# Six stages of a float32 transformer kernel take their first two output pairs by halves of the inputs

## The chip, the cores and the metric

One core of one Trainium2 chip runs the whole program in one launch. The metric is the device time of one execution in microseconds, as the median of several; lower is better.

## The reference

Batch 1, 256 tokens, width 2048, all in float32. A first block of two layers, then a second block of one layer. Cut to the matrix products, which are most of the work (`rms` is a root-mean-square norm):

```python
for l in range(2):                                   # first block
    proj = rms(x) @ w_in[l]                          # 56 tiles of 128 columns
    mixed = [short_gated_conv(...), diff_attention(...), memory_attention(mem @ w_mem_kv[l])]
    x = x + concat(mixed) @ w_out[l]
# second block
h = rms(x) * (1 + sc1) + sh1                         # modulation: silu(c) @ w_mod + b_mod
proj = h @ w_in_2
o_a = sliding_window_attention(...); o_b = gated_linear_attention(...)
merged = sigmoid(g_a) * (o_a @ w_branch_attn) + sigmoid(g_b) * (o_b @ w_branch_gla)
x = x + g1 * rms(merged @ w_out_2)
h = rms(x) * (1 + sc2) + sh2
x = x + g2 * rms((silu(gate) * val) @ w_down)        # gate, val = conv(h @ w_up)
```

## The kernel before, in words

**Stages, pairs, units.** Every matrix product is a stage. They run one after another: mem0, mem1, qkv0, heads0a to c, out0, qkv1, heads1a to c, out1, q_a, and so on to g_b, branch_a, branch_b, mix_out, up0, down0, up1, down1. A stage makes its output in pairs of tiles. A pair needs all 16 tiles of the input, and takes them in `per_pair` steps. One step is a unit: 512 KB of weights (`UK` = 4 input tiles by 256 output columns; in a token stage `WK` = 2 input tiles by 512 columns) and the matmuls on them. mem1, out0, qkv1 and branch_b have 4 units to a pair; out1 and mix_out are token stages, in which the input is the stationary operand, with 8. A turn is `body` = 2 pairs (in token stages the loop goes over pairs directly).

**Float32 from halves.** Each float32 value is split into a rounded high part and the rest. The weights of a unit land in `RAW`; ScalarE writes the high part `WH` (`act_split`, L540), VectorE the rest `WL` (`dve_split`, L549), and TensorE multiplies (L468 and L473; in token stages L415 to L417). ScalarE and VectorE split four units ahead: at unit w of a stage, `split_ahead` splits unit w+4, into one of `RING` = 4 slots, once unit w is done. The count of splits goes by the unit's place in the stage.

**Input chunks.** The input `XH` of a stage is prepared in four chunks of four tiles (`act_input_chunk`, L1121 and L1127; `dve_input_chunk`, L1138 and L1146). `xh_ready` counts them, and TensorE waits for chunk q in the first pair only, at unit q (at units 2q and 2q+1 in a token stage). The first chunks are prepared beside the last units of the stage before (`inside`), the others behind its last evacuation.

**Banks and evacuation.** Pairs alternate between two halves of the accumulator `ACC` in PSUM: an even pair uses banks 0 and 1, an odd one banks 2 and 3. At the end of a pair ScalarE copies one part to `HIGH` (L804), and VectorE adds (L938 and L940; L950, L953, L956, L961 in the stages with a sum), which raises `evacuated`. A pair may start when the pair two before it is evacuated:

```python
wait_from_zero(pe, k.evacuated, i * stage.body + (stage.pair0 + b - 1))   # first unit of pair b
```

**Order.** Each engine has its program written out in order; all run the same loop over pairs and units, and each does for unit w its split ahead, its side work for that place (sums, memory keys at L1473, attention of another stage, a modulation step L1932 on VectorE), and at a pair's end the evacuation. SP issues the loads of weights (`RAW`) and of modulation (`RAWMOD`) in one fixed sequence, five buffers deep: a load waits until the one five before it is used. In mem1 the column sums of four chunks (L1084) stand behind unit 1, in qkv1 those of the last chunk (L1061) behind unit 3.

Of the kernel before, what the change touches and what calls it, by code (L numbers as in the profile page):

```python
# [11 lines left out]
P = 128  # L12
# [20 lines left out]
NORMED = ("out1", "mix_out", "down1")  # L33
WARM = 32
# [63 lines left out]
class Stage:  # L98


    def __init__(self, name, source, per_pair, pairs, body, inputs, kind, dst, tiles=2,
# [12 lines left out]
        assert pairs % body == 0 and self.units % RING == 0  # L114

# [172 lines left out]

def end_unit(stage):

    return stage.unit0 + stage.pairs * stage.per_pair
# [15 lines left out]
def wait_from_zero(engine, sem, value):  # L307

    if value > 0:
        engine.wait_ge(sem, value)  # L310

# [8 lines left out]
def program_sync(sp, k):  # L320
# [73 lines left out]
def pe_token_stage(pe, k, stage):  # L394

    operand = k.AH if stage.inputs is None else k.XH
    for j in range(stage.pairs):
        bank0 = 2 * ((stage.pair0 + j) % 2)
        pe.wait_ge(k.evacuated, stage.pair0 + j - 1)
        if stage.name == "mix_out" and j > 1:  # L400
            pe.wait_ge(k.tok_squared, 8 + 2 * (j - 1))
        for q in range(stage.per_pair):
            w = j * stage.per_pair + q
            if stage.inputs is not None and j == 0:
                pe.wait_ge(k.xh_ready, stage.inputs + q * WK // UK + 1)
            if stage.inputs is None and j == 0:
                pe.wait_ge(k.evacuated, stage.pair0 - WK * (stage.per_pair - q - 1))
            pe.wait_ge(k.split_ready, stage.unit0 + w + 1)
            high, low = wide(k.WH[:, w % RING]), wide(k.WL[:, w % RING])
            for b in range(2):  # L410
                bank = k.ACC[:, bank0 + b]
                for kc in range(WK):
                    tile = WK * q + kc
                    x = operand[:, tile, b * P:b * P + P]
                    pe.matmul(bank, x, high[:, kc], start=tile == 0, stop=False)  # L415
                    pe.matmul(bank, x, low[:, kc], start=False, stop=False)  # L416
                    mm = pe.matmul(bank, operand[:, tile, T + b * P:T + b * P + P], high[:, kc],  # L417
                                   start=False, stop=tile == WK * stage.per_pair - 1)
                if b == 0 and q == stage.per_pair - 1:
                    mm.then_inc(k.half_done, 1)  # L420
            mm.then_inc(k.unit_done, 1)
            pe_beside(pe, k, stage, j, q)
            if stage.name == "out1" and (j, q) == (1, 7):
                pe_rotary(pe, k)
            if stage.name == "down1" and j == 0 and q in (1, 3, 5, 7):
                pe_gain_rows(pe, k, 1, q // 2)
# [21 lines left out]
def pe_stage(pe, k, stage):  # L448
# [27 lines left out]
    def turn(i, last):  # L476
        for b in range(stage.body):
            bank0 = 2 * ((stage.pair0 + b) % 2)

            wait_from_zero(pe, k.evacuated, i * stage.body + (stage.pair0 + b - 1))  # L480
            if stage.name == "up0" and (i, b) == (0, 0):
                pe_first_tiles(pe, k, stage)
                continue
            for q in range(stage.per_pair):
                w = b * stage.per_pair + q
                by_tile = stage.inputs in (k.plan.h2, k.plan.f_in)
                if stage.inputs is not None and b == 0 and not by_tile:
                    pe.wait_ge(k.xh_ready, stage.inputs + q + 1)
                if stage.inputs is None and b == 0:
                    pe.wait_ge(k.evacuated, stage.pair0 - UK * (stage.per_pair - q - 1))  # L490
                pe.wait_ge(k.split_ready, i * stage.units + (stage.unit0 + w + 1))
                for n in range(0, UK * stage.tiles, 2):
                    both = [operands(bank0, q, n + a) for a in range(2)]
                    if stage.name == "q_a" and (i, b) == (0, 0):
                        if both[0][3] + 4 < KT:
                            pe_turn_normed(pe, k, 0, both[0][3] + 4)
                        pe.wait_ge(k.xh_ready, stage.inputs + both[1][3] + 1)
                    high(both[0], w)
                    high(both[1], w)
                    low(both[0], w)  # L500
                    mm = low(both[1], w)
                mm.then_inc(k.unit_done, 1)
                pe_beside(pe, k, stage, i, w)
                if stage.name == "mem0" and (i, w) == (0, 5):
                    pe.wait_ge(k.consts_ready, 1)
                    for c in range(4):
                        presummed_sums(pe, k, 0, c)
                if stage.name == "mem1" and (i, w) == (0, 1):
                    pe.wait_ge(k.rstd_ready, 1)
                    for c in range(4):  # L510
                        presummed_sums(pe, k, 1, c)
                if stage.name == "mem1" and (i, w) == (0, 3):
                    pe_memory_keys(pe, k, 0)
                if stage.name == "qkv0" and (i, w) == (0, 5):
                    pe_memory_keys(pe, k, 1)
                if stage.name == "qkv0" and (i, w) == (1, 1):
                    pe.wait_ge(k.mk_ready, 2)
                if stage.name == "qkv1" and i > 0 and w == 1:
                    pe_turn_residual(pe, k, i - 1)
                if stage.name == "kv_a" and w == 1:  # L520
                    pe_decays(pe, k)
                if stage.name == "g_b" and w == 5:
                    pe_gain_rows(pe, k, 0, i)
                if stage.norm is not None and b % 2 == 1 and q == 1 and i * stage.body + b > 1:
                    presummed_sums(pe, k, stage.norm, (i * stage.body + b) // 2 - 1)
                if stage.sums_last is not None and w == 3 and i == 0:
                    chunk_sums(pe, k, stage.sums_last, 3)
# [35 lines left out]
def act_token_stage(act, k, stage, chain):  # L563

    for j in range(stage.pairs):
        last_pair = j == stage.pairs - 1
        for q in range(stage.per_pair):
            w = j * stage.per_pair + q
            late = stage.name in ("out1", "mix_out") and last_pair and q == stage.per_pair - 1
            if not late:  # L570
                token_split_ahead(act, k, stage, w, act_split)
            act_beside(act, k, stage, j, q, chain)
            if stage.name == "out1" and (j, q) == (2, 5):
                act_rotary(act, k)
            if stage.name == "down1" and j == 0 and q in (2, 4, 6, 8):
                act_gain_rows(act, k, 1, q // 2 - 1)
        if stage.name == "down0":
            continue
# [1920 lines left out]
```

## Time and profile before

| | us |
|---|---|
| median of 3 runs | 2597.96 |
| lowest and highest | 2597.32, 2598.81 |
| span of the profiled execution, first to last instruction | 2596.0 |
| TensorE busy in it | 2547.3 |
| VectorE busy in it | 1939.5 |
| ScalarE busy in it | 1300.1 |

The profile is of one execution. It gives the span of that execution and no other time for it, so its own time is at least the 2596.0 us of the span; the median of the runs is 1.96 us above that. The granted clock of TensorE, averaged over the span, is 0.995 of full speed. A matmul's end is modelled, and matmuls overlap, so the start times are what to go by.

### The profile page before, as it was taken

Reading aid. Unit: us, or ns where it says so; the run is one execution under the profiler, and the core shown is the slowest. Engines: PE = TensorE matmul, PEld = TensorE weight load, DVE = VectorE, ACT = ScalarE, POOL = GpSimd, SP = SyncE. Lnnn points to the kernel's source line nnn. Section 1 sums busy time; section 2 is a strip of 40 time slices with the busy share of each in tenths; the row PEclk is TensorE's granted clock in tenths of the full one; section 3 lists DMA queues with packets and bytes.
Section 4 is the critical chain, followed back from the end, with each engine's and each line's share of the span. In section 5 each row is a group of like instructions: output and inputs, shape, how many; then the busy total and the mean of one; then the engine's idle time right before and its main releaser. Section 6 shows DMA issues by size and latency. Waiting matters only on the chain.

```text
span 2596.0 us, 35319 instructions
## 1 busy us (share of the span) xinstructions
PE 2547.3 (98%) x13936; PEld 2175.1 (84%) x13936; DVE 1939.5 (75%) x2769; ACT 1300.1 (50%) x1758; POOL 10.8 (0%) x62
## 2 busy tenths in 40 slices
PE   7999999999999999999999999999999999999998
PEld 6888888888888887888788888888888888888886
DVE  6877766887777687676667787887788887788855
ACT  7544555554455555454444554544644443444443
POOL 0000000000000010000000000000000000000000
PEclk9999999999999999999999999999999999999999
DMA  8687554778754466755567788888476668976764
GB/s 271 219 299 244 160 154 143 228 258 286 242 158 152 149 214 218 235 171 154 153 190 222 231 277 277 270 282 272 143 197 189 188 208 307 284 203 196 201 194 140
DMA packets 526519, 556.64 MB, mean 214 GB/s; under 512 B 17409, under 2 KB 453762, under 8 KB 526226
## 3 DMA queue, kind: packets, MB, share of 16 engines
q1 hardware_dynamic: 526354, 554.38, 68.4%
q8 instruction: 110, 1.80, 0.3%
q14 instruction: 55, 0.45, 0.1%
HBM read 552.22 MB, written 2.10 MB: 214 GB/s over the span
## 4 chain that ended last, share of the span: by engine, by line
PE 88%; DVE 7%; ACT 3%; issue 1%; DMA 0%; DVEq 0%; SPq 0%; ACTq 0%
PE ACC L468 43%; PE ACC L473 21%; PE ACC L415 6%; PE ACC L417 6%; PE ACC L416 6%; DVE WL L549 2%; PE OU L1268 1%; ACT WH L540 1%; PE SC L1235 1%; PE SC L1247 1%; ACT PROB L1293 1%; PE SC L1276 1%; DVE XH L1138 0%; DVE XH L1146 0%; DVE PROB L1352 0%
## 5 line engine op out<-in xcount | busy, mean ns | idle before, releaser
L468 PE MATMUL ACC<-XH,WH 128*128 128x512 f32 x5296 | 1692.3, 401 | 21.2 <-DVE XH L1146 15.3
L540 ACT ACTIVATE WH<-RAW 128x1024 fp32r<-128x1024 f32 (+1 forms) x852 | 897.9, 1057 | 1166.5 <-PE ACC L473 836.1
L549 DVE TENSOR_TENSOR WL<-RAW,WH 128x1024 fp32r<-128x1024 f32 (+1 forms) x852 | 1032.6, 1220 | 568.5 <-ACT WH L540 567.0
L473 PEld LDWEIGHTS ACC<-XH,WL 128*128 128x128 f32 x5296 | 998.7, 189 | 236.6
L473 PE MATMUL ACC<-XH,WL 128*128 128x256 f32 x5296 | 1044.2, 279 | 0.0
L468 PEld LDWEIGHTS ACC<-XH,WH 128*128 128x128 f32 x5296 | 814.4, 189 | 41.2 <-issue 18.5
L1932 DVE SCALAR_TENSOR_TENSOR RAWMOD<-RAWMOD,CSILU 128x1024 f32<-128x1024 f32 x192 | 233.8, 1218 | 1.0 <-DMA RAWMOD<-in_w_mod_t 0.7
L415 PE MATMUL ACC<-WH,XH 128*128 128x512 f32 x384 | 151.9, 396 | 3.6 <-DVE WL L549 3.6
L416 PE MATMUL ACC<-WL,XH 128*128 128x512 f32 x384 | 149.6, 390 | 0.0
L417 PE MATMUL ACC<-WH,XH 128*128 128x512 f32 x384 | 149.5, 389 | 0.0
L415 PE MATMUL ACC<-WH,AH 128*128 128x512 f32 x352 | 137.3, 390 | 0.0
L417 PE MATMUL ACC<-WH,AH 128*128 128x512 f32 x352 | 137.0, 389 | 0.0
L416 PE MATMUL ACC<-WL,AH 128*128 128x512 f32 x352 | 137.0, 389 | 0.0
L415 PEld LDWEIGHTS ACC<-WH,XH 128*128 128x128 f32 x384 | 72.1, 188 | 22.1 <-issue 7.5
L804 ACT ACTIVATE HIGH<-ACC 128x512 f32<-128x512 f32 (+1 forms) x171 | 89.9, 526 | 0.0
L417 PEld LDWEIGHTS ACC<-WH,XH 128*128 128x128 f32 x384 | 72.1, 188 | 15.3
L416 PEld LDWEIGHTS ACC<-WL,XH 128*128 128x128 f32 x384 | 72.1, 188 | 14.4
L417 PEld LDWEIGHTS ACC<-WH,AH 128*128 128x128 f32 x352 | 66.1, 188 | 13.8
L416 PEld LDWEIGHTS ACC<-WL,AH 128*128 128x128 f32 x352 | 66.1, 188 | 13.5
L415 PEld LDWEIGHTS ACC<-WH,AH 128*128 128x128 f32 x352 | 66.1, 188 | 13.5
L938 DVE TENSOR_TENSOR PR<-ACC,HIGH 128x512 f32<-128x512 f32 x64 | 43.7, 682 | 3.6 <-ACT HIGH L804 3.6
L979 DVE SCALAR_TENSOR_TENSOR CV<-U,PARAM,CV 128x256 f32<-128x256 f32 x88 | 42.7, 485 | 3.1
(287 smaller groups left out, 1438.0 us busy)
## 6 DMA issues: line engine op xcount, KB each, us to landing
RAW<-in_w_in SPq DMA_DIRECT2D x408, 512.0 KB, 4.5
RAWMOD<-in_w_mod_t SPq DMA_DIRECT2D x192, 512.0 KB, 4.9
RAW<-in_w_up SPq DMA_DIRECT2D x176, 512.0 KB, 4.7
RAW<-in_w_out SPq DMA_DIRECT2D x96, 512.0 KB, 5.4
RAW<-in_w_down SPq DMA_DIRECT2D x88, 512.0 KB, 5.0
RAW<-in_w_mem_kv SPq DMA_DIRECT2D x32, 512.0 KB, 5.8
RAW<-in_w_branch_gla SPq DMA_DIRECT2D x32, 512.0 KB, 5.1
RAW<-in_w_branch_attn SPq DMA_DIRECT2D x16, 512.0 KB, 5.2
```

The lines of the kernel that those rows point to most:

```text
L415: pe.matmul(bank, x, high[:, kc], start=tile == 0, stop=False)
L416: pe.matmul(bank, x, low[:, kc], start=False, stop=False)
L417: mm = pe.matmul(bank, operand[:, tile, T + b * P:T + b * P + P], high[:, kc], start=False, stop=tile == WK * stage.per_pair - 1)
L468: return pe.matmul(bank, k.WH[:, w % RING, kc, cols], x, start=tile == 0, stop=False)
L473: return pe.matmul(bank[:, 0:T], k.WL[:, w % RING, kc, cols], x[:, 0:T], start=False, stop=tile == tiles - 1)
L540: act.activation(k.WH[:, slot, :, 0:width], k.RAW[:, r % RAWS, :, 0:width], ACT.Copy).then_inc(k.hi_ready, 1)
L549: dve.tensor_tensor(k.WL[:, slot, :, 0:width], k.RAW[:, k.plan.unit_load[unit] % RAWS, :, 0:width], k.WH[:, slot, :, 0:width].bitcast(F32) ...
L804: act.activation(k.HIGH[:, first:stage.tiles], k.ACC[:, bank + first:bank + stage.tiles, T:2 * T], ACT.Copy).then_inc(k.high_ready, 1)
L938: chain.link(dve.tensor_tensor(dst, low, high, ALU.add))
L979: dve.scalar_tensor_tensor(out=cv, in0=u[:, 0:T], scalar=column(taps[0]), in1=cv, op0=ALU.mult, op1=ALU.add).then_inc(done, 1)
L1235: mm = pe.matmul(k.SC[:, c, b * T:b * T + T], q, keys, start=True, stop=True)
L1932: dve.scalar_tensor_tensor(out=raw, in0=raw, scalar=1.0, in1=k.CSILU[:, half * MOD_COLS:(half + 1) * MOD_COLS], op0=ALU.mult, op1=ALU.mult ...
```

## The change

A list names six stages. In each, the first two pairs go by halves of their units: first half of pair 0, first half of pair 1, second half of pair 0, second half of pair 1. Later pairs go as before. All engines and the loads follow the same order. What is done at a place in the stage (the w-th unit: splits, sums, memory keys, modulation) stays at that place; what is done at a pair's end (the copy to `HIGH`, the evacuation) moves with the pair: for the first pair from behind unit 3 to behind unit 5 (token stages: from 7 to 11); the second pair's stays behind unit 7 (15). TensorE's wait for `evacuated` stands at each pair's first unit.

```diff
+HALVED = ("mem1", "out0", "qkv1", "out1", "branch_b", "mix_out")
...
+    def order(self):
+
+        if self.name not in HALVED:
+            return [(b, q) for b in range(self.body) for q in range(self.per_pair)]
+        half = self.per_pair // 2
+        return [(b, part * half + q) for part in range(2) for b in range(2) for q in range(half)]
...
+def stage_order(stage):
+
+    order = stage.order()
+    done = len(order) // stage.per_pair
+    return order + [(j, q) for j in range(done, stage.pairs) for q in range(stage.per_pair)]
+
+
+def pair_end(stage, j):
+
+    return stage.unit0 + stage_order(stage).index((j, stage.per_pair - 1)) + 1
...
+def turn_order(stage, i):
+
+    return stage.order() if i == 0 else [(b, q) for b in range(stage.body)
+                                         for q in range(stage.per_pair)]
...
     for stage in k.stages:
-        for j in range(stage.pairs):
-            for q in range(stage.per_pair):
-                by_unit[stage.unit0 + j * stage.per_pair + q] = (stage, j, q)
+        for w, (j, q) in enumerate(stage_order(stage)):
+            by_unit[stage.unit0 + w] = (stage, j, q)
...
     operand = k.AH if stage.inputs is None else k.XH
-    for j in range(stage.pairs):
+    for w, (j, q) in enumerate(stage_order(stage)):
         bank0 = 2 * ((stage.pair0 + j) % 2)
-        pe.wait_ge(k.evacuated, stage.pair0 + j - 1)
...
+        if q == 0:
+            pe.wait_ge(k.evacuated, stage.pair0 + j - 1)
...
     def turn(i, last):
...
+        for w, (b, q) in enumerate(turn_order(stage, i)):
             bank0 = 2 * ((stage.pair0 + b) % 2)
...
+            if q == 0:
+                wait_from_zero(pe, k.evacuated, i * stage.body + (stage.pair0 + b - 1))
...
+            if stage.inputs is not None and b == 0 and not by_tile:
+                pe.wait_ge(k.xh_ready, stage.inputs + q + 1)
...
+            pe.wait_ge(k.split_ready, i * stage.units + (stage.unit0 + w + 1))
...
+    def copy_high(i, b):
...
+        act.wait_ge(k.unit_done, pair_end(stage, i * stage.body + b))
...
+            if q == stage.per_pair - 1:
+                copy_high(i, b)
...
+            if q == stage.per_pair - 1:
+                evacuate(i, b)
```

TensorE's order at the head of mem1, from the end of unit 1 over the column sums into unit 2. The name in brackets is what a row waits for. Before:

```order
L468 MATMUL ACC<-XH,WH 128x512 x2
L473 MATMUL ACC<-XH,WL 128x256 x2
L1084 MATMUL OU<-PR,ONES 128x256 [waits presummed,rstd_ready]
L1084 MATMUL OU<-PR,ONES 128x256 [waits presummed] x3
L468 MATMUL ACC<-XH,WH 128x512 [waits split_ready,xh_ready]
L468 MATMUL ACC<-XH,WH 128x512
```

And now (the file's lines have moved, L492 is the former L468, L1115 the former L1084):

```order
L492 MATMUL ACC<-XH,WH 128x512 x2
L497 MATMUL ACC<-XH,WL 128x256 x2
L1115 MATMUL OU<-PR,ONES 128x256 [waits presummed,rstd_ready]
L1115 MATMUL OU<-PR,ONES 128x256 [waits presummed] x3
L492 MATMUL ACC<-XH,WH 128x512 [waits split_ready,evacuated]
L492 MATMUL ACC<-XH,WH 128x512
```

Unit 2 belonged to the first pair and waited for an input chunk; it now belongs to the second pair and waits for that pair's bank.

VectorE's order in out0 from the splits of its units 4 and 5 on: WL rows are splits, RAWMOD rows modulation steps, the SUM and X rows a pair's evacuation. Before:

```order
L549 TENSOR_TENSOR WL<-RAW,WH 128x1024 [waits hi_ready] x2
L1932 SCALAR_TENSOR_TENSOR RAWMOD,DERIVED<-RAWMOD,CSILU 128x1024 [waits landed3]
L549 TENSOR_TENSOR WL<-RAW,WH 128x1024 [waits hi_ready] x2
L1932 SCALAR_TENSOR_TENSOR RAWMOD,DERIVED<-RAWMOD,CSILU 128x1024 [waits landed1]
L950 TENSOR_TENSOR SUM<-ACC,HIGH 128x512 [waits high_ready]
L961 TENSOR_TENSOR X<-X,SUM 128x512 [waits dve_step]
L549 TENSOR_TENSOR WL<-RAW,WH 128x1024 [waits hi_ready] x2
L1932 SCALAR_TENSOR_TENSOR RAWMOD,DERIVED<-RAWMOD,CSILU 128x1024 [waits landed4]
L549 TENSOR_TENSOR WL<-RAW,WH 128x1024 [waits hi_ready] x2
```

And now (L573 is the former L549, L1963 the former L1932, L982 and L993 the former L950 and L961):

```order
L573 TENSOR_TENSOR WL<-RAW,WH 128x1024 [waits hi_ready] x2
L1963 SCALAR_TENSOR_TENSOR RAWMOD,DERIVED<-RAWMOD,CSILU 128x1024 [waits landed3]
L573 TENSOR_TENSOR WL<-RAW,WH 128x1024 [waits hi_ready] x2
L1963 SCALAR_TENSOR_TENSOR RAWMOD,DERIVED<-RAWMOD,CSILU 128x1024 [waits landed1]
L573 TENSOR_TENSOR WL<-RAW,WH 128x1024 [waits hi_ready] x2
L1963 SCALAR_TENSOR_TENSOR RAWMOD,DERIVED<-RAWMOD,CSILU 128x1024 [waits landed4]
L982 TENSOR_TENSOR SUM<-ACC,HIGH 128x512 [waits high_ready]
L993 TENSOR_TENSOR X<-X,SUM 128x512 [waits dve_step]
L573 TENSOR_TENSOR WL<-RAW,WH 128x1024 [waits hi_ready] x2
```

The first pair's evacuation has moved behind two more splits (units 8 and 9) and one more modulation step.

## Rows read from the trace of the kernel before

**Rows 1.** The page: span, busy time (share) and instructions; two costliest split groups

```profile
span 2596.0 us, 35319 instructions
...
PE 2547.3 (98%) x13936; PEld 2175.1 (84%) x13936; DVE 1939.5 (75%) x2769; ACT 1300.1 (50%) x1758; POOL 10.8 (0%) x62
...
L540 ACT ACTIVATE WH<-RAW 128x1024 fp32r<-128x1024 f32 (+1 forms) x852 | 897.9, 1057 | 1166.5 <-PE ACC L473 836.1
L549 DVE TENSOR_TENSOR WL<-RAW,WH 128x1024 fp32r<-128x1024 f32 (+1 forms) x852 | 1032.6, 1220 | 568.5 <-ACT WH L540 567.0
```

**Rows 2.** TensorE's waits, whole span: released by, us in total, times, longest

```profile
PE ACC L468 <- DVE XH L1146: 15.3, 3, 11.1
...
PE ACC L415 <- DVE WL L549: 3.6, 2, 2.8
```

**Rows 3.** Timeline of TensorE, head of qkv1: start, us, row, idle before and releaser

```profile
567.00 0.63 PE L468 MATMUL ACC<-XH,WH 128*128 128x512 f32 x2
...
569.78 0.63 PE L468 MATMUL ACC<-XH,WH 128*128 128x512 f32 x2
...
575.14 0.73 PE L468 MATMUL ACC<-XH,WH 128*128 128x512 f32 x2 [2.41 <-DVE XH L1146]
...
579.60 1.89 PE L1061 MATMUL SC<-PR,ONES 128*128 128x256 f32 x8
581.13 0.81 PE L468 MATMUL ACC<-XH,WH 128*128 128x512 f32 x2
```

**Rows 4.** Timeline of TensorE, out0: starts of units 2, 3 and 4

```profile
477.23 0.63 PE L468 MATMUL ACC<-XH,WH 128*128 128x512 f32 x2
...
481.97 0.73 PE L468 MATMUL ACC<-XH,WH 128*128 128x512 f32 x2 [1.80 <-DVE XH L1138]
...
484.87 0.63 PE L468 MATMUL ACC<-XH,WH 128*128 128x512 f32 x2
```

**Rows 5.** Timeline of VectorE, out0

```profile
477.33 0.69 DVE L940 TENSOR_TENSOR PR<-PR,RSTD 128x512 f32<-128x512 f32 x1
...
483.00 2.36 DVE L549 TENSOR_TENSOR WL<-RAW,WH 128x1024 fp32r<-128x1024 f32 x2 [1.08 <-ACT WH L540]
...
491.68 2.60 DVE L549 TENSOR_TENSOR WL<-RAW,WH 128x1024 fp32r<-128x1024 f32 x2
494.19 1.22 DVE L1932 SCALAR_TENSOR_TENSOR RAWMOD<-RAWMOD,CSILU 128x1024 f32<-128x1024 f32 x1
```

**Rows 6.** Timeline of TensorE, mem1: unit 1, the sums, unit 2

```profile
66.40 0.73 PE L468 MATMUL ACC<-XH,WH 128*128 128x512 f32 x2 [1.77 <-DVE XH L1146]
...
70.85 1.89 PE L1084 MATMUL OU<-PR,ONES 128*128 128x256 f32 x8
72.39 0.81 PE L468 MATMUL ACC<-XH,WH 128*128 128x512 f32 x2
```

**Rows 7.** Timeline of VectorE: last evacuations before mem1 and before qkv1

```profile
74.54 0.69 DVE L940 TENSOR_TENSOR PR<-PR,RSTDM 128x512 f32<-128x512 f32 x1
...
570.95 0.69 DVE L961 TENSOR_TENSOR X<-X,SUM 128x512 f32<-128x512 f32 x1
```

**Rows 8.** Timelines of VectorE and TensorE, out1, unit 4 and its split

```profile
941.01 2.36 DVE L549 TENSOR_TENSOR WL<-RAW,WH 128x1024 fp32r<-128x1024 f32 x2 [1.07 <-ACT WH L540]
...
942.38 0.47 PE L415 MATMUL ACC<-WH,XH 128*128 128x512 f32 x1 [2.77 <-DVE WL L549]
```

**Rows 9.** Windows: length, busy (count) of PE, PEld, DVE, ACT, POOL; PEclk, DMA share, GB/s

```profile
67.30:70.70 3.40, 3.40 (x12) 2.81 (x11) 3.33 (x8) 1.56 (x3) 0.00 (x0) 0.50 0.44 154
...
575.90:579.30 3.40, 3.40 (x12) 2.90 (x12) 3.40 (x5) 1.27 (x2) 0.00 (x0) 0.50 0.43 127
```

**Rows 10.** Timelines around branch_b: last evacuation before it, unit 2, a modulation step

```profile
1665.94 0.69 DVE L953 TENSOR_TENSOR PR<-PR,SUM 128x512 f32<-128x512 f32 x1
...
1668.25 0.63 PE L468 MATMUL ACC<-XH,WH 128*128 128x512 f32 x2
...
1681.89 1.22 DVE L1932 SCALAR_TENSOR_TENSOR RAWMOD<-RAWMOD,CSILU 128x1024 f32<-128x1024 f32 x1
```

More of the change, by code:

```diff
@@ L396, in pe_token_stage @@
     operand = k.AH if stage.inputs is None else k.XH
-    for j in range(stage.pairs):
+    for w, (j, q) in enumerate(stage_order(stage)):
         bank0 = 2 * ((stage.pair0 + j) % 2)
-        pe.wait_ge(k.evacuated, stage.pair0 + j - 1)
-        if stage.name == "mix_out" and j > 1:
+        if q == 0:
+            pe.wait_ge(k.evacuated, stage.pair0 + j - 1)
+        if q == 0 and stage.name == "mix_out" and j > 1:
             pe.wait_ge(k.tok_squared, 8 + 2 * (j - 1))
[L402 to L426, printed above, removed]
@@ L429, in pe_first_tiles @@
+        mm.then_inc(k.unit_done, 1)
+        pe_beside(pe, k, stage, j, q)
+        if stage.name == "out1" and (j, q) == (1, 7):
+            pe_rotary(pe, k)
+        if stage.name == "down1" and j == 0 and q in (1, 3, 5, 7):
+            pe_gain_rows(pe, k, 1, q // 2)
 def pe_first_tiles(pe, k, stage):
@@ L476, in turn @@
     def turn(i, last):
-        for b in range(stage.body):
+        if stage.name == "up0" and i == 0:
+            pe.wait_ge(k.evacuated, stage.pair0 - 1)
+            pe_first_tiles(pe, k, stage)
+        for w, (b, q) in enumerate(turn_order(stage, i)):
             bank0 = 2 * ((stage.pair0 + b) % 2)
-            wait_from_zero(pe, k.evacuated, i * stage.body + (stage.pair0 + b - 1))
             if stage.name == "up0" and (i, b) == (0, 0):
-                pe_first_tiles(pe, k, stage)
                 continue
[L484 to L527, printed above, removed]
@@ new lines, in turn @@
+            for n in range(0, UK * stage.tiles, 2):
+                both = [operands(bank0, q, n + a) for a in range(2)]
+                if stage.name == "q_a" and (i, b) == (0, 0):
+                    if both[0][3] + 4 < KT:
+                        pe_turn_normed(pe, k, 0, both[0][3] + 4)
+                    pe.wait_ge(k.xh_ready, stage.inputs + both[1][3] + 1)
+                high(both[0], w)
+                high(both[1], w)
+                low(both[0], w)
+                mm = low(both[1], w)
@@ new lines, in turn @@
+            mm.then_inc(k.unit_done, 1)
+            pe_beside(pe, k, stage, i, w)
+            if stage.name == "mem0" and (i, w) == (0, 5):
+                pe.wait_ge(k.consts_ready, 1)
+                for c in range(4):
+                    presummed_sums(pe, k, 0, c)
+            if stage.name == "mem1" and (i, w) == (0, 1):
+                pe.wait_ge(k.rstd_ready, 1)
+                for c in range(4):
+                    presummed_sums(pe, k, 1, c)
+            if stage.name == "mem1" and (i, w) == (0, 3):
+                pe_memory_keys(pe, k, 0)
@@ L529, in pe_stage @@
+            if stage.sums_last is not None and w == 3 and i == 0:
+                chunk_sums(pe, k, stage.sums_last, 3)
     stage_turns(stage, turn)
@@ new lines, in dve_token_stage @@
+        late = stage.name in ("out1", "mix_out") and last_pair and q >= stage.per_pair - 2
+        if not late:
+            token_split_ahead(dve, k, stage, w, dve_split)
+        unit = stage.unit0 + w
+        if unit in k.plan.mod_adds:
+            dve_modulation_sums(dve, k, k.plan.mod_adds[unit], chain)
+        for n in k.plan.mod_steps.get(unit, ()):
+            dve_modulation(dve, k, n)
+        dve_beside(dve, k, stage, j, q, chain)
+        if stage.name == "out1" and (j, q) == (1, 5):
+            dve_rotary(dve, k)
```

331 lines of the change are left out of this document (173 added, 158 removed).

## The prediction

> **What bounds the kernel now.** I read the page first: TensorE is busy for 98% of the span [rows 1], so only its gaps, its clock and work put on its path can move the time. Then the list of who waited for whom for TensorE: it waited for input chunks (VectorE's XH) and for weight splits (VectorE's WL) [rows 2]; 11.1 us of the first is the start of the program. Then TensorE's timeline at the head of each of the six stages, beside VectorE's. A unit takes 2.79 us: two neighbours start at 567.00 and 569.78 [rows 3]. I number a stage's units from 0. The waits at the heads are:
> - mem1, unit 1: 1.77 us [rows 6].
> - out0, unit 3: 1.80 us [rows 4].
> - qkv1, unit 3: 2.41 us [rows 3].
> - out1, unit 4: 2.77 us [rows 8], and mix_out, unit 4: the rest of the 3.6 us that two waits for WL make, 0.8 us [rows 2].
>
> A gap can cost twice. After the waits of 1.77 and 2.41 us the granted clock was 0.50 (1.2 GHz) for 3.4 us [rows 9]. In qkv1 unit 3 ran from 575.14 to the column sums at 579.60, so 4.46 us where 2.79 are normal: 1.67 us lost [rows 3].
>
> **What the change does to each head.** Unit 0 and 1 stay the first pair's. Units 2 and 3 become the second pair's first half, 4 and 5 the first pair's second half. Two things follow. Input chunks 2 and 3 are wanted two units later, in token stages four. But the second pair's bank is wanted two units earlier, so unit 2 now waits until the last pair of the stage before is evacuated.
>
> *mem1.* Unit 2 started at 72.39, right behind eight sum matmuls from 70.85; it waited for nothing [rows 6]. The wait of unit 1 is for chunk 1, which the new order still wants there. So nothing is removed. What is added: the last pair of mem0 is evacuated by VectorE's L940, which starts at 74.54 and takes 0.69 us, so it ends at 75.23 [rows 7]. Unit 2 starts about 75.25 in place of 72.39, 2.86 us later. Of that some 0.1 us comes back, since unit 2 of before was still slowed at its start. Cost: **+2.75 us**, and nothing behind takes it up: the later heads' chunks and evacuations wait for TensorE's own units, so they move along with it.
>
> *out0.* Unit 2 would start at 477.23 [rows 4]; the bank is free when L940, from 477.33, has ended at 478.02 [rows 5]: 0.8 us of new wait. Units 2 and 3 then end at 478.05 + 2 x 2.79 = 483.63. Unit 4 needs no late chunk, but its weights: VectorE's split starts at 483.00, and of the two in 2.36 us the first ends about 484.2 [rows 5]. Unit 4 so starts at 484.2, not at 484.87 [rows 4]: 0.67 us gained, not 1.80. Then unit 8, the third pair, wants the first pair's bank. That pair now ends with unit 5 and not 3, and VectorE reaches its evacuation behind two splits from 491.68 and the modulation step of 494.19 (1.22 us), so from 495.33; two steps of 0.69 us end at 496.7 [rows 5]. Unit 8 would start at 484.2 + 4 x 2.79 = 495.36, and before it was 484.87 + 11.16 = 496.03. So it starts at 496.7: **+0.7 us** over before. The 0.67 us are given back, and the same again.
>
> *qkv1.* Unit 2 would start at 569.78 [rows 3]; out0's last evacuation, L961 from 570.95, ends at 571.64 [rows 7]. New wait 1.9 us. Unit 3 follows at 574.5, by when chunk 3 is not wanted; the sums come at 577.3 and take 1.53 us (579.60 to 581.13), unit 4 starts at 578.8 in place of 581.13 [rows 3]. **-2.35 us**: 0.7 because a wait of 1.9 stands for one of 2.6 between starts, 1.67 from the clock, if that stays at 2.4 GHz. At unit 8 the first pair's evacuation is in time: behind unit 5 come a ScalarE split of 1.06, a VectorE split of 1.22 [rows 1] and two steps of 0.69, 3.7 us, where two units give 5.58.
>
> *out1.* Unit 4 waits for its split, not for a chunk: VectorE's WL rows start at 941.01, the first ends about 942.2, and TensorE goes on at 942.38 [rows 8]. Weights are split by the unit's place in the stage, whichever pair it serves. The wait stays whole: **0**. *mix_out* is the same with 0.8 us [rows 2]: **0**.
>
> *branch_b.* Its late chunks are 0 and 1, wanted at units 0 and 1 in either order. The bank for unit 2 is free at 1666.63 (L953) [rows 10], and unit 2 started at 1668.25: no wait. At unit 8, due at 1668.25 + 6 x 2.79 = 1685.0, VectorE has the modulation step of 1681.89 (1.22 us) and then three evacuation steps of some 0.7 us: 1685.2 [rows 10]. **+0.25 us**.
>
> No instruction, byte or DMA is added; the loads are the same number in the same places of SP's queue, only with other columns. I cost that at 0; a stall would show as ScalarE's splits waiting for DMA.
>
> Sum at full clock: 2.75 + 0.7 - 2.35 + 0 + 0 + 0.25 = +1.35 us.
>
> **The clock.** The change makes two new waits, about 2.5 us in mem1 and 1.9 us in qkv1. Of the four waits of this size that I listed, those of 1.77 and 2.41 us were followed by half clock, those of 1.80 and 2.77 us were not [rows 3, 4, 6, 8, 9]. So each new one costs 0 or 1.67 us, and I take one of the two: +1.67. Forecast: +3.0 us over the median of 2597.96, so **2601.0 us**. The sum is made against the profiled execution with its span of 2596.0 us [rows 1]; the median of the three runs is 1.96 us above that span, and I carry that over. A measurement here can tell a change of about 0.2%, 5.2 us, from none.
>
> The Trainium skill's page "TensorE: Matmul & The Clock Gate", section "HAM oscillation — how this bites in real kernels", advises to do all K-tiles of one output tile before waiting, so that TensorE stays warm. [...]
>
> **The rivals.**
> - *Both new waits are followed by half clock*: +1.35 + 2 x 1.67 = +4.7, 2602.7 us. For it: 2.5 us is longer than two waits that were followed by it. Against it: 2.77 us in out1 was not. Or *neither is*: 2599.3 us. [...]
> - *The heads' waits simply vanish* (faster). Then 1.80 + 2.41 + 1.67 + 2.77 + 0.8 = 9.45 us go: 2588.5 us. For it: all these waits stand at units that the change moves. Against it: out1's and mix_out's are for splits, and the two evacuations above lie later than the units that now want them. It holds only if both readings are wrong.
> - *The first pair's evacuation is late at unit 8 in more stages* (slower). VectorE works in order, and the evacuation now has two units of room, 5.58 us, where it had four. In mem1 its queue also holds the memory keys and a modulation step there, in branch_b it is late already. One more VectorE step of 1.2 us in front of it in mem1, qkv1 and branch_b makes 3.6 us: +1.35 + 3.6 + 1.67 = 6.6, 2604.6 us. It decides as soon as the queue is behind by more than the 1.8 us that qkv1 has to spare.
> - That the order is not what the diff says: the listings show it is. No chance given.
>
> **How the numbers follow.** One half-clock period more: 0.35; both: 0.20; neither: 0.15; all three lie within 5.2 us of before. Vanishing waits: 0.10. Late evacuations: 0.20. So faster 0.10, same 0.70, slower 0.20. The range leaves out the vanishing waits (0.1) and the worse half of the late evacuations (0.1): it goes up to 2604.6. Down it goes to 2596.0: 2599.3, less 1.67 if mem1's own half-clock period goes too, less the 1.5 us by which the three runs differ.
>
> **What would show it.** In the changed kernel's profile: at mem1's head a TensorE wait of about 2.5 us released by the evacuation (PR, the former L940) behind the sums, and the old 1.8 us before it; in out0 three short waits (0.8 for PR, 0.5 for WL, 1.3 for X before unit 8) in place of one; in qkv1 1.9 us for X before unit 2 and none before unit 5; out1 and mix_out still 2.8 and 0.8 us for WL. The number of half-clock periods decides within 3.3 us. I am wrong if mem1 shows no wait for PR, or if the WL wait of out1 is gone.

## The result, and the profile of the changed kernel

The changed kernel took 2604.46 us (median of 7 runs, 2601.96 to 2606.76), the kernel before beside it 2597.64 us (7 runs, 2597.14 to 2598.81): a ratio of 1.0022, interval 1.0013 to 1.0031. That is 6.8 us more, where 3.0 were forecast: the sign was right, the size was not. The profiled execution took 2604.52 us, with a span of 2602.8 us against 2596.0 [rows 1].

The page of the changed kernel, its first lines:

```profile
span 2602.8 us, 35319 instructions
...
PE 2551.4 (98%) x13936; PEld 2177.3 (84%) x13936; DVE 1940.0 (75%) x2769; ACT 1300.1 (50%) x1758; POOL 10.8 (0%) x62
```

The number of instructions is that of before, and VectorE's and ScalarE's busy times are within 0.5 us of it. TensorE alone is busy 4.1 us longer with the same matmuls, and the other 2.7 us are gaps. TensorE's waits of the changed kernel over the whole span (released by, us in total, times, longest), those of its unit streams:

```profile
PE ACC L492 <- DVE XH L1177: 12.7, 2, 11.0
...
PE ACC L439 <- DVE WL L573: 3.6, 2, 2.8
...
PE ACC L492 <- DVE PR L972: 3.2, 2, 2.5
PE ACC L492 <- DVE X L993: 3.1, 2, 1.8
```

Beside [rows 2]: the chunk waits (XH) have lost qkv1's 2.4 us and out0's 1.8 us, and what is left is the program's start and mem1's 1.7. The split waits (WL) of out1 and mix_out are whole, 3.6 us. New are waits for evacuated banks: 3.2 us for PR, 3.1 us for X. TensorE's timeline at the heads (start, us, row, idle before and releaser):

```profile
70.70 1.89 PE L1115 MATMUL OU<-PR,ONES 128*128 128x256 f32 x8
75.12 0.73 PE L492 MATMUL ACC<-XH,WH 128*128 128x512 f32 x2 [2.53 <-DVE PR L972]
...
480.71 0.73 PE L492 MATMUL ACC<-XH,WH 128*128 128x512 f32 x2 [0.69 <-DVE PR L972]
...
487.02 0.70 PE L492 MATMUL ACC<-XH,WH 128*128 128x512 f32 x2 [0.46 <-DVE WL L573]
...
499.74 0.73 PE L492 MATMUL ACC<-XH,WH 128*128 128x512 f32 x2 [1.34 <-DVE X L993]
...
575.53 1.07 PE L492 MATMUL ACC<-XH,WH 128*128 128x512 f32 x2 [1.75 <-DVE X L993]
...
582.77 1.89 PE L1092 MATMUL SC<-PR,ONES 128*128 128x256 f32 x8
584.31 0.81 PE L492 MATMUL ACC<-XH,WH 128*128 128x512 f32 x2
...
945.53 0.47 PE L439 MATMUL ACC<-WH,XH 128*128 128x512 f32 x1 [2.78 <-DVE WL L573]
```

These waits stand at the units where the prediction had put them: mem1 unit 2, out0 units 2, 4 and 8, qkv1 unit 2, out1 unit 4. In branch_b no wait is listed; unit 8 starts at 1691.65 us, right behind the third evacuation step of 1690.90 (0.69 us). To read what each head costs I took the time from the start of one unit to the next in both traces and summed the differences of a head:

| head | forecast | changed less before |
|---|---|---|
| mem1 | +2.75 | +2.7 |
| out0 | +0.7 | +1.1 |
| qkv1 | -2.35 | -0.7 |
| out1, mix_out | 0 | 0.0 |
| branch_b | +0.25 | +0.3 |
| kv_a | not listed | +3.2 |

They sum to 6.6 of the 6.8 us. Two lines are off by more than half a microsecond, and they are both the clock. In qkv1 the new wait was followed by half clock as the old one was. And kv_a, a stage that the change does not touch, took 3.2 us more in its units 1 and 2. There TensorE does sixteen 16-row matmuls for the decays, in the changed kernel:

```profile
1088.85 1.99 PE L1715 MATMUL SC<-GKL,WUP 16*128 16x256 f32 x8
1090.68 3.16 PE L1715 MATMUL OU<-GKL,WUP 16*128 16x256 f32 x8
1093.77 1.22 PE L492 MATMUL ACC<-XH,WH 128*128 128x512 f32 x2
```

and in the kernel before:

```profile
1085.64 1.99 PE L1684 MATMUL SC<-GKL,WUP 16*128 16x256 f32 x8
1087.48 1.89 PE L1684 MATMUL OU<-GKL,WUP 16*128 16x256 f32 x8
1089.29 0.72 PE L468 MATMUL ACC<-XH,WH 128*128 128x512 f32 x2
```

The first eight are alike, the second eight take 1.81 us before and 3.09 after, from their start to that of the next row. The same window in both (length, busy (count) of PE, PEld, DVE, ACT, POOL; PEclk, DMA share, GB/s), of the changed kernel:

```profile
1091.20:1097.90 6.70, 6.70 (x20) 5.07 (x19) 0.13 (x1) 0.00 (x0) 0.00 (x0) 0.50 0.52 167
```

and of the kernel before:

```profile
1091.20:1097.90 6.70, 6.70 (x40) 5.85 (x40) 4.36 (x9) 1.06 (x1) 0.00 (x0) 1.00 0.31 88
```

At a clock of 0.50, against 1.00 (1.2 GHz against 2.4), TensorE does 20 matmul records in 6.7 us and not 40. Nothing had it waiting ahead of that: it was at work all through, on matmuls with 16 rows. So the question for the runs was whether the change brings this about, or chance does.

### The profile page after: what moved, and what is told of

It is laid out like the page before. It is cut to its first block, busy times and chain, and to the rows that moved or that the text cites. A ratio compares the mean times of both kernels' runs of the same rounds, so it can differ in the third digit from the quotient of the medians.

```text
span 2602.8 us, 35319 instructions
## 1 busy us (share of the span) xinstructions
PE 2551.4 (98%) x13936; PEld 2177.3 (84%) x13936; DVE 1940.0 (75%) x2769; ACT 1300.1 (50%) x1758; POOL 10.8 (0%) x62
## 4 chain that ended last, share of the span: by engine, by line
PE 87%; DVE 8%; ACT 3%; issue 1%; DMA 0%; DVEq 0%; SPq 0%; ACTq 0%
PE ACC L492 43%; PE ACC L497 21%; PE ACC L439 6%; PE ACC L441 6%; PE ACC L440 6%; DVE WL L573 2%; ACT WH L564 1%; PE OU L1299 1%; PE SC L1266 1%; PE SC L1278 1%; ACT PROB L1324 1%; PE SC L1307 1%; DVE XH L1177 0%; DVE RAWMOD L1963 0%; DVE PROB L1383 0%
## 5 line engine op out<-in xcount | busy, mean ns | idle before, releaser
L492 PE MATMUL ACC<-XH,WH 128*128 128x512 f32 x5296 | 1694.3, 401 | 23.8 <-DVE XH L1177 12.7
L573 DVE TENSOR_TENSOR WL<-RAW,WH 128x1024 fp32r<-128x1024 f32 (+1 forms) x852 | 1032.9, 1220 | 575.9 <-ACT WH L564 574.3
L492 PEld LDWEIGHTS ACC<-XH,WH 128*128 128x128 f32 x5296 | 815.4, 190 | 45.0 <-issue 19.5
L1963 DVE SCALAR_TENSOR_TENSOR RAWMOD<-RAWMOD,CSILU 128x1024 f32<-128x1024 f32 x192 | 233.9, 1218 | 2.8 <-DMA RAWMOD<-in_w_mod_t 2.7
L1009 DVE SCALAR_TENSOR_TENSOR CV<-U,PARAM,CV 128x256 f32<-128x256 f32 x88 | 42.7, 485 | 3.1
L1011 DVE SCALAR_TENSOR_TENSOR CV<-U,PARAM,CV 128x256 f32<-128x256 f32 x88 | 42.7, 485 | 3.1
```

The lines of the kernel that those rows point to most:

```text
L492: return pe.matmul(bank, k.WH[:, w % RING, kc, cols], x, start=tile == 0, stop=False)
L573: dve.tensor_tensor(k.WL[:, slot, :, 0:width], k.RAW[:, k.plan.unit_load[unit] % RAWS, :, 0:width], k.WH[:, slot, :, 0:width].bitcast(F32) ...
L1009: chain.link(dve.scalar_tensor_tensor(out=cv, in0=u[:, 1:1 + T], scalar=column(taps[1]), in1=cv, op0=ALU.mult, op1=ALU.add))
L1011: dve.scalar_tensor_tensor(out=cv, in0=u[:, 0:T], scalar=column(taps[0]), in1=cv, op0=ALU.mult, op1=ALU.add).then_inc(done, 1)
L1963: dve.scalar_tensor_tensor(out=raw, in0=raw, scalar=1.0, in1=k.CSILU[:, half * MOD_COLS:(half + 1) * MOD_COLS], op0=ALU.mult, op1=ALU.mult ...
```

## The experiments

**A count of half-clock periods.** A trace records the granted clock. In all of them it falls to 0.50 for 3.4 us at a time (or 6.8, two such periods in a row, as in kv_a above), and a period costs about 1.7 us of TensorE's work. I counted them in each trace, leaving out the one at the program's end and what of a period lies ahead of mem1's wait for its bank, where it costs nothing (shown below), and took 1.7 us for each off the span:

| kernel | span | periods that cost | span less 1.7 each |
|---|---|---|---|
| before | 2596.0 | 6 | 2585.8 |
| before, again | 2597.2 | 7 | 2585.3 |
| changed | 2602.8 | 7 (and 1 free) | 2590.9 |
| changed, again | 2595.7 | 3 (and 1 free) | 2590.6 |
| mem1 alone | 2597.7 | 5 | 2589.2 |
| mem1 alone, bank early | 2597.7 | 5.9 (and 0.1 free) | 2587.7 |
| qkv1 alone | 2596.7 | 7 | 2584.8 |
| out0, branch_b alone | 2603.3 | 9 | 2588.0 |
| out1, mix_out alone | 2600.9 | 9 | 2585.6 |
| before, decays in two parts | 2593.9 | 5 | 2585.4 |
| changed, decays in two parts | 2601.1 | 6.4 (and 0.6 free) | 2590.2 |
| before, early splits | 2593.2 | 6 | 2583.0 |
| early splits, two halved stages | 2589.7 | 5 | 2581.2 |

The count is good to about 1 us. It leaves in that the program starts unevenly: mem1's unit 1 starts at 65.07 us in the earliest of these traces and at 66.87 in the latest (66.40 and 65.47 in the two of the kernel before). And it takes off 1.7 us where a period runs partly into some other wait.

The runs that made these traces follow.

**Both kernels again, on another chip.** The changed kernel as it is, timed:

> The changed kernel itself, timed beside the kernel before on this chip. My theory: +3.3 us at full clock, as in its first profile, and half-clock periods that fall differently in each execution of either kernel: medians 2 to 7 us apart, both with a spread of 5 us or more. Rival (the 6.8 us of the first measurement belong to the change): 6 to 7.5 us apart again, and half clock behind kv_a's small matmuls again.

2601.98 us (11 runs, 2597.37 to 2604.79) against 2598.31 (21 runs, 2595.59 to 2602.3): 1.0008, interval 0.9999 to 1.0017. Its profiled execution, of the very program of above, has a span of 2595.7 us, shorter than the 2596.0 of the kernel before. In it neither new wait was followed by half clock: qkv1's units 2 and 3 start 2.91 us apart, where they are 4.45 apart in the execution shown first (575.53 and 579.98). The windows in mem1's unit 1, behind mem1's new wait, and in kv_a:

```profile
66.50:69.70 3.20, 3.20 (x12) 2.79 (x11) 3.13 (x7) 1.76 (x3) 0.00 (x0) 0.50 0.50 161
...
75.20:78.40 3.20, 3.20 (x20) 2.79 (x20) 3.20 (x4) 0.54 (x1) 0.00 (x0) 1.00 0.04 2
...
1087.00:1090.30 3.30, 3.30 (x11) 2.82 (x11) 0.00 (x0) 0.00 (x0) 0.00 (x0) 0.50 0.51 158
```

and the starts of qkv1's units 2 and 3:

```profile
574.82 0.74 PE L492 MATMUL ACC<-XH,WH 128*128 128x512 f32 x2 [1.76 <-DVE X L993]
...
577.73 0.63 PE L492 MATMUL ACC<-XH,WH 128*128 128x512 f32 x2
```

The medians are 3.7 us apart and both spreads over 6 us, as expected; the +3.3 us at full clock was too low, by the count it is 5.3.

The kernel before, unchanged, one more execution:

> The kernel before, a second profile. My theory: same start-to-start steps at all heads, but other half-clock periods than the six of the first profile, by chance of when the gaps fall, and a span that differs by 1.7 us for each one more or less. Rival: the same six at the same places.

2598.96 us with a span of 2597.2. Its kv_a had half clock too, which it had not had in the execution that I forecast from:

```profile
1086.20:1089.50 3.30, 3.30 (x9) 2.17 (x8) 0.00 (x0) 0.00 (x0) 0.00 (x0) 0.50 0.67 217
```

Four of its periods stand where those of the first execution did (here at 413.7, 574.1, 871.1 and 1021.3 us), mem1's is gone, and kv_a's is new. So kv_a's cost is not the change's. Of the ten traces with the sixteen matmuls in one block (both kernels, with every choice of halved stages) nine show half clock there, and the one that does not is the execution that I forecast from. With the periods taken off, the two executions of each kernel agree within 0.5 us (2585.8 and 2585.3; 2590.9 and 2590.6), though their spans differ by 1.2 and 7.1. By the count the change itself costs some 5.2 us, and the execution shown first had one costly period more than before's: 5.2 + 1.7 = 6.9, where 6.8 were measured. On this second chip the medians differ by 3.7 us, and the interval does not exclude zero.

**The heads one by one.** Four kernels, each the changed one with fewer stages halved, all beside the same runs of the kernel before: 2599.17 us (33 runs, 2596.95 to 2604.8).

```
-HALVED = ("mem1", "out0", "qkv1", "out1", "branch_b", "mix_out")
+HALVED = ("mem1",)
...
+HALVED = ("qkv1",)
...
+HALVED = ("out0", "branch_b")
...
+HALVED = ("out1", "mix_out")
```

*mem1 alone:*

> Only mem1 goes by halves. My theory: unit 2 waits about 2.5 us for the last evacuation of mem0, all later work moves by 2.75 us, so about +2.7 us over before, plus 0 to 3.3 us of half-clock periods that fall otherwise because the later events have moved. Rival (the waits of the head are what counts): no more than 0.3 us, since no wait is added that the chunks did not make.

2603.34 us (11 runs), 1.0010, interval 1.0001 to 1.0018: 4.2 us more. TensorE's waits from 60 to 95 us:

```profile
PE ACC L492 <- DVE PR L972: 4.1, 1, 4.1
PE ACC L492 <- DVE XH L1177: 1.8, 1, 1.8
```

The chunk wait is still there, as forecast, and the bank wait behind it is 4.1 us, where the changed kernel had 2.53. The reason is in its timeline: the sums, unit 2, and the matmuls of the memory keys' squares, a mark two units on:

```profile
68.29 1.89 PE L1115 MATMUL OU<-PR,ONES 128*128 128x256 f32 x8
74.28 0.73 PE L492 MATMUL ACC<-XH,WH 128*128 128x512 f32 x2 [4.11 <-DVE PR L972]
...
81.54 1.88 PE L1504 MATMUL SC<-MKSQ,ONES 128*128 128x512 f32 x4
```

The sums start at 68.29, in the changed kernel at 70.70: here unit 1 ran at full clock. Unit 2 starts at 74.28 and 75.12, behind the same evacuation, since VectorE gets there at its own time. In the kernel before, its second execution had unit 1 at full clock too:

```profile
68.37 1.89 PE L1084 MATMUL OU<-PR,ONES 128*128 128x256 f32 x8
70.31 0.73 PE L468 MATMUL ACC<-XH,WH 128*128 128x512 f32 x2
...
76.01 1.88 PE L1473 MATMUL SC<-MKSQ,ONES 128*128 128x512 f32 x4
```

Unit 2 starts 4.0 us later (74.28 less 70.31), and the mark 5.5 us later (81.54 less 76.01): behind the bank wait comes half clock. Here is this kernel's window there:

```profile
75.20:78.40 3.20, 3.20 (x13) 2.69 (x12) 3.20 (x4) 0.00 (x0) 0.00 (x0) 0.55 0.11 16
```

So mem1 costs 2.7 us against an execution whose unit 1 is slow, since the halved order waits for VectorE either way and a full clock ahead of that wait buys nothing; against one whose unit 1 is not slow it costs 4.0, and with a period behind the bank wait 5.5. Five traces have mem1 halved. In two of them unit 1 was slow and unit 2 was not, in the other three it was the other way round. (In the changed kernel with the decays in two parts, below, half clock lasted 6.8 us, the first 2.0 of them in the bank wait, and mem1 cost 6.2.) Of the eight traces without mem1 halved four have a period in mem1. That a halved mem1 paid one way or the other in all five fits its 4.2 us, between the 2.7 and the 5.5.

*qkv1 alone:*

> Only qkv1 goes by halves. My theory: a wait of 1.9 us before unit 2 stands for the wait of 2.6 us before unit 3, so -0.7 us, and -2.35 us if no half-clock period follows it. Rival (the chunk wait vanishes): no wait in the head, -2.4 us at half clock before and up to -4.1 us.

2600.21 us, 1.0000, interval 0.9992 to 1.0009. TensorE's timeline at unit 2, its only wait from 560 to 590 us:

```profile
569.52 0.73 PE L492 MATMUL ACC<-XH,WH 128*128 128x512 f32 x2 [1.77 <-DVE X L993]
```

A wait of 1.8 us for the bank stands for one of 2.4 for the chunk. The count puts it 0.5 to 1.0 us under the kernel before; the time can't tell. This new wait too was followed by half clock, from 570.4 us on.

*out0 and branch_b alone:*

> Only out0 and branch_b go by halves. My theory: out0 loses 0.7 to 1.1 us, since unit 8 waits for the first pair's late evacuation, and branch_b 0.25 us in the same way: +1.0 to +1.4 us. Rival (the chunk wait of out0 vanishes): -1.8 us.

2597.84 us, 0.9999, interval 0.9989 to 1.0008. TensorE's waits from 470 to 505 us:

```profile
PE ACC L492 <- DVE X L993: 1.6, 1, 1.6
PE ACC L492 <- DVE PR L972: 0.7, 1, 0.7
PE ACC L492 <- DVE WL L573: 0.5, 1, 0.5
```

Three waits of 2.8 us in all in place of one of 1.8. Its profiled execution has nine half-clock periods and is the longest of the four, while its median is no longer than before's. By the count it costs 2.2 to 2.7 us, but it is the trace with one of the latest starts (mem1's unit 1 at 66.73). From unit start to unit start it costs 1.4 us in out0 and 0.3 in branch_b, 1.7 in all, a little over the 1.0 to 1.4 expected; no interval here shows it.

*out1 and mix_out alone:*

> Only the token stages out1 and mix_out go by halves. My theory: unit 4 waits for its weight split in either order, waits of 2.8 and 0.8 us stay, 0.0 us within 0.3. Rival (the waits are for chunks): -3.6 us.

2597.84 us, 1.0001, interval 0.9992 to 1.0011, and the count gives 0 as well. TensorE's wait in out1 (925 to 1000 us), and in mix_out (1750 to 1800 us):

```profile
PE ACC L439 <- DVE WL L573: 2.8, 1, 2.8
...
PE ACC L439 <- DVE WL L573: 0.8, 1, 0.8
```

Both waits for the split are untouched by the order of the pairs.

**The bank by itself.** mem1 alone, and the last pair of mem0 evacuated one step earlier, ahead of mem1's input chunk in VectorE's queue:

```
             if last and b == stage.body - 1 and q < stage.inside and stage.then:
+                if stage.name == "mem0" and q == stage.per_pair - 1:
+                    evacuate(i, b)
                 dve_input_chunk(dve, k, k.preps[stage.then], q)
-            if q == stage.per_pair - 1:
+            if q == stage.per_pair - 1 and not (stage.name == "mem0" and last and b == 1):
                 evacuate(i, b)
```

> Only mem1 goes by halves, and VectorE evacuates the last pair of mem0 ahead of input chunk 3 instead of behind it. My theory (unit 2 waits for the bank): unit 2 waits until some 1.6 us earlier, so about 0.9 to 1.0 us in place of 2.5, and the head loses 1.2 us in place of 2.8. Rival (unit 2 waits for something else, as its split): the wait stays 2.5 us.

2600.95 us, 1.0009, interval 1.0000 to 1.0018. The evacuation and unit 2:

```profile
72.07 0.69 DVE L972 TENSOR_TENSOR PR<-PR,RSTDM 128x512 f32<-128x512 f32 x1
...
72.81 1.22 PE L492 MATMUL ACC<-XH,WH 128*128 128x512 f32 x2 [2.52 <-DVE PR L972]
```

In the kernel with mem1 alone the same evacuation step started at 73.54. It comes 1.5 us sooner and the wait is 1.6 us shorter, 2.5 for 4.1. So it is the bank, and not the chunk, the weights or the sums, that holds unit 2. The gain is the expected one, the level is not: a wait of 1.0 us was expected and 2.5 measured, since the 2.5 that I started from were those of an execution with a slow unit 1. Each over its own before, the two kernels take 3.2 and 4.2 us more, and by the count 2.1 and 3.7; the intervals of the ratios overlap, so the times alone don't show the gain.

**The decays in two parts.** To see what kv_a's half clock hangs on, its sixteen matmuls go eight behind unit 1 and eight behind unit 2, in the changed kernel, and in the kernel before:

```
-            if stage.name == "kv_a" and w == 1:
-                pe_decays(pe, k)
+            if stage.name == "kv_a" and w in (1, 2):
+                pe_decays(pe, k, w - 1)
...
-    for t in range(GLA_T):
+    for t in range(GLA_T // 2 * part, GLA_T // 2 * (part + 1)):
...
-        dve.wait_ge(k.decay_logits, 1)
+        dve.wait_ge(k.decay_logits, 2)
```

> The changed kernel, with the sixteen 16-row matmuls of kv_a in two parts, eight behind unit 1 and eight behind unit 2. My theory: the 3.2 us lost in kv_a in the changed kernel are half-clock periods that follow these 3.7 us of small matmuls by chance of when they fall; apart they are never followed by one, so no half clock at 1080 to 1100 us and a median 1.5 to 3.2 us below the changed kernel's. Rival (the change itself slows kv_a): no difference.

> The kernel before, with the sixteen 16-row matmuls of kv_a in two parts, as in the run above. My theory: the kernel before loses up to 3.2 us there in some executions too; here in none, so the highest times (2601 to 2605 us) go and the median is 0 to 3 us lower. Rival (it is the change's doing): same median and same spread as before.

Beside 2597.76 us (28 runs, 2595.92 to 2604.62) the changed one took 2600.24 (1.0005, interval 0.9996 to 1.0014), the one before 2597.47 (0.9996, interval 0.9988 to 1.0005). The window over kv_a, changed kernel with the decays in two parts:

```profile
1085.00:1097.00 12.00, 12.00 (x64) 9.73 (x63) 5.37 (x6) 4.26 (x5) 0.00 (x0) 1.00 0.84 271
```

and the kernel before with them:

```profile
1078.00:1090.00 12.00, 12.00 (x64) 9.74 (x62) 5.37 (x6) 4.25 (x5) 0.00 (x0) 1.00 0.87 276
```

Full clock in both, and in the last kernel below, which has the two parts as well: three traces of three, where nine of ten with one block had half clock. So the block goes with it, as far as three traces can show; what it is about the block (its length, the matmuls of 16 rows) stays open. What that is worth the times don't show: 0.3 us under before, inside the interval, where one or two periods would be 1.7 to 3.4. The highest times did not go either (2601.88 and 2601.63 are among the eleven). The changed kernel as it was did not run beside these, so the 1.5 to 3.2 us expected of the first of the two can't be read off.

**The waits that the order can't reach.** out1's and mix_out's waits are for VectorE's split of the unit four places on, which it reaches too late. In the kernel before (no stage halved) that split is taken up ahead of the stage's last preparation steps, for out0, out1 and mix_out:

```
+EARLY = ("out0", "out1", "mix_out")
 def split_ahead(engine, k, stage, i, w, last, split):
+    if stage.name in EARLY and (i, w) == (0, 0):
+        return
...
 def dve_mix_end(dve, k, l):
+    dve_split(dve, k, k.plan.s[f"out{l}"], 0, RING)
...
     stage_turns(stage, turn)
+    if stage.name == "branch_b":
+        dve_split(dve, k, stage.next, 0, RING)
```

with the same three edits for the token stages and ScalarE.

> Every stage pair by pair, as before; only the early split of unit 4 in out0, out1 and mix_out. My theory: out1 and mix_out lose their waits of 2.8 and 0.8 us, out0's chunk 3 comes some 0.4 us later: 3.2 to 3.5 us less than before at full clock. Rival (the halves are needed for that gain): the waits stay at unit 4 or go to unit 6, 0 us.

2594.82 us (11 runs, 2591.86 to 2597.69) against 2598.31: 0.9985, interval 0.9976 to 0.9994. out1's unit 4, where 2.77 us were waited [rows 8]:

```profile
941.06 0.47 PE L439 MATMUL ACC<-WH,XH 128*128 128x512 f32 x1 [0.42 <-DVE WL L573]
```

mix_out has no such wait. 2.4 + 0.8 = 3.2 us of waits went and 3.5 us of time (2.3 to 2.8 by the count), from edits of order alone. The wait for out0's chunk 3 grew by 0.35 us, to 2.15.

**A version that takes the parts that pay.** Only out0 and qkv1 halved, the early splits, the decays in two parts, and in out0 the first pair evacuated ahead of the split that stood before it (the other edits are those above):

```
+HALVED = ("out0", "qkv1")
...
+            early_pair = stage.name == "out0" and (i, w) == (0, 5)
+            if early_pair:
+                evacuate(i, b)
             split_ahead(dve, k, stage, i, w, last, dve_split)
```

> Only out0 and qkv1 go by halves; in out0, out1 and mix_out ScalarE and VectorE split unit 4 before the stage's chunk 3 instead of behind it, out0's first pair is evacuated ahead of the split of unit 9, and kv_a's small matmuls are apart. My theory: the wait of 2.8 us in out1 and of 0.8 us in mix_out vanish though both go pair by pair, since they were for the split; out0 gains 1.2 us over before, qkv1 0.7 us or more; 5 to 6 us less than before at full clock, and up to 3 us more by kv_a. Rival (the waits at unit 4 are for the input): they stay, and the time is 1 to 2 us below before.

2590.63 us (6 runs, 2588.8 to 2591.44) against 2597.76: 0.9970, interval 0.9959 to 0.9982. TensorE's waits over the whole span, those of its unit streams:

```profile
PE ACC L492 <- DVE X L1005: 1.8, 1, 1.8
...
PE ACC L492 <- DVE PR L984: 0.7, 1, 0.7
...
PE ACC L439 <- DVE WL L573: 0.4, 1, 0.4
```

The third pair of out0 no longer waits for its bank (X, 1.34 us in the changed kernel), and mem1 has its old single wait. It is 7.1 us under the kernel before (4.1 to 4.6 by the count, so some of it is periods that it happened not to have) and beats both. How much of that each part gives was not tried apart, but for the early splits' 3.5.

## Why the prediction was right or wrong

**What bounds the kernel.** Right. TensorE's share stayed at 98%, and the 6.8 us are its gaps and its clock, nothing else: VectorE's and ScalarE's busy times did not move.

**mem1, +2.75.** Measured at 2.7 in the execution shown first, and the wait for PR came as described, 2.53 us long, behind the sums. The term was bound to the execution, though: I read unit 2's start of 72.39 [rows 6] as the kernel's, and it was that of an execution slowed in unit 1, which four of eight traces without the change here are. Against the others the cost is 4.0 us, and 5.5 with a period behind the new wait. By the single-stage runs mem1 carries what can be measured of the change: 4.2 us alone, and the other three show no difference.

**out0, +0.7.** Measured 1.1, and 0.75 between the second executions of the two kernels. All three waits came (0.69, 0.46 and 1.34 us against 0.8, 0.5 and 1.3 in the forecast's list). But one step of the chain came out right by luck. I had the splits from 491.68 and the modulation step from 494.19 [rows 5] as fixed, though the change takes the two evacuation steps ahead of them (490.33 to 491.74) away, so VectorE could have been there 1.35 us sooner. It was not, since it waited for ScalarE, and ScalarE for the weights. In the changed kernel, VectorE's splits, modulation step and X step, then ScalarE's split:

```profile
494.62 2.59 DVE L573 TENSOR_TENSOR WL<-RAW,WH 128x1024 fp32r<-128x1024 f32 x2 [1.23 <-ACT WH L564]
497.13 1.22 DVE L1963 SCALAR_TENSOR_TENSOR RAWMOD<-RAWMOD,CSILU 128x1024 f32<-128x1024 f32 x1
...
498.99 0.69 DVE L993 TENSOR_TENSOR X<-X,SUM 128x512 f32<-128x512 f32 x1
...
493.53 1.06 ACT L564 ACTIVATE WH<-RAW 128x1024 fp32r<-128x1024 f32 x1 [5.08 <-DMA RAW<-in_w_out]
```

From 497.13 to the end at 499.68 are 2.55 us, and I had 2.5 (494.19 to 496.7). The start lies 2.94 us later, 2.7 of them mem1's and the rest the weights'. ScalarE's splits did wait for DMA here, 3.91 us before and 5.08 after; I had named that as the sign of a stall and costed the loads at 0. Without the 1.23 us that VectorE lost by it most of the 1.34 us at unit 8 would go, an estimate from these rows.

**qkv1, -2.35.** The 0.7 from the shorter wait are there. The 1.67 for the clock are not, in this execution: the period came behind the new wait. In the second one it did not, and there qkv1 took 2.2 us less than in the second of the kernel before, which had its period. The sum held the gain in one term and, in the next, one of two new waits "followed by half clock", so it had counted on this; but it then left no room for a period without a wait.

**out1, mix_out, 0, and branch_b, +0.25.** Right, at 0.0 and 0.3; branch_b's evacuation ends at 1691.59 us and unit 8 starts at 1691.65. The waits of 2.78 and 0.8 us are for splits and did not move. The rival of vanishing waits was rightly refused by that reading, and the last experiments show it from the other side: the same waits go when the split goes earlier.

**The clock, +1.67.** This is the step that failed. "So each new one costs 0 or 1.67 us" counted half clock at the new waits alone, and took every other period as fixed. In the execution shown first, mem1's new wait was not followed by it and qkv1's was, so one of two, as I had taken; in its second execution neither was. But the periods of the whole program are not fixed: 6 and 7 that cost in the kernel before, 7 and 3 in the changed one, 5 to 9 in the others. kv_a's two, 3.2 of the 6.8 us, stand behind no wait at all, and the execution that I read was the one in ten without them. Four more of the six of before (at 415.5, 872.9 and, two in a row, 1023.1 us) lie outside the heads that I had read, and they too stand right behind waits of TensorE. In the list of waits of the kernel before, whose ends are at 415.01, 871.95 and 1022.51 us (the second group's other wait is 1.3 us long):

```profile
PE OU L1268 <- ACT TURNED L1307: 4.5, 2, 2.3
PE SC L726 <- DVE PR L911: 4.2, 2, 2.9
```

So "two of four" was a rate from part of the waits: of the seven of 1.7 to 2.9 us that another engine ended, five were followed by half clock, at that rate the likelier outcome for each new wait, and for the wait that qkv1 lost as well.

In sum: without the clock the unit starts give 4.0 + 1.1 - 0.7 + 0.3 = 4.7 us, and the count 5.2; the forecast had 2.75 + 0.7 - 0.7 + 0.25 = 3.0. Most of that difference is mem1's 1.3. The clock adds one period of 1.7, where the forecast's two clock terms, -1.67 in qkv1 and +1.67 for a new wait, came to nothing.

**Both new waits at half clock.** I gave this 0.20. The changed kernel's first execution shows one, its second none, the one with the decays in two parts both. For mem1 that was too little: in all five traces with mem1 halved half clock falls on its first wait or on its second. The Trainium skill's page "TensorE: Matmul & The Clock Gate" (section "HAM oscillation — how this bites in real kernels") advises, for a thin matmul that waits for a DMA at every K-tile (here, an input tile), to do all K-tiles of an output tile before waiting. Its case is not this one. Here doing otherwise cost nothing by the unit (2.79 us in both orders); what it cost was the earlier need of the bank, and the clock behind that wait in three traces of five.

**The late evacuations,** the slower rival at 2604.6 us, have the measured time of 2604.46 and not its mechanism: no wait at a unit 8 of mem1 or qkv1 stands in the list of waits. A time near a forecast proves nothing of the cause.

**The range and the chances.** 2596.0 to 2604.6 held 2604.46, by a little. "Slower by over 0.2%" had a chance of 0.2, and the first comparison gives 0.22%; the second chip gives 0.14% between the medians and 0.08% as the ratio of its runs, which is the case that had 0.7. So the case given 0.20 stands for the first chip, narrowly, with an interval (1.0013 to 1.0031) that lies on both sides of 0.2%.

## What to carry to other kernels

An order that visits more output tiles early wants their PSUM banks early: before counting which input waits it removes, look up when the bank's last owner is evacuated, in the queue of the engine that does it. Read the start that a new wait is measured against in more than one execution, since the one at hand may have been slow just there. For changes under 0.2% compare executions after taking off the half-clock periods, and give the clock terms of the whole program a spread, not only those at the places you touch. Take the rate at which a wait is followed by half clock from all waits of the program, not from those at hand.

## What the runs showed of the hardware that I had not expected

- The granted clock falls to 0.50 for 3.4 us at a time, 8 and 4 times in two executions of one program, with spans of 2602.8 and 2595.7 us. This alone is as much as the whole difference measured.
- But for kv_a's it falls at the same few waits of TensorE, more often at some than at others, and not by their length: at the wait of 2.88 us near 1020 us in all 13 traces, at those of 2.26 us near 415 and 872 us in 12 and 10, at the first of mem1 (1.77 us) in 6, at out1's of 2.8 us in 4 of the 11 that have it. Why some are hit more often stays open.
- It falls in kv_a with TensorE busy throughout, in or behind sixteen matmuls of 16 rows (nine traces of ten; eight such matmuls take 1.8 us at full clock, 3.1 us where it falls), and not with two blocks of eight (none of three).
- A half-clock period ahead of a wait for another engine costs nothing: mem1's unit 2 starts at 74.28 us where unit 1 was fast and at 75.12 where it was slow, and these 0.84 us are there at unit 1's own start already (65.39 and 66.23), while the sums start 2.4 us apart.
